# Second block's mixer: token-major values, pool means on GpSimd, heads 0 and 1 first, a place for each head's attention weights

## What is computed

```python
h = rmsnorm(x, mix_norm[l])
p = h @ w_in[l]                                   # 1024 -> 2048
a, f = p[..., :256], p[..., 256:512]              # pool, Fourier
q = p[..., 512:1024]; k = p[..., 1024:1536]       # 4 heads x 2 x 64
v = p[..., 1536:]                                 # 4 heads x 128

# pool: mean over a window of w in (2, 4, 8, 16) tokens for each 64 columns, minus the token itself
outs.append(win_sum / cnt - af[:, :, g])
y_pool = einsum('bsgc,gcd->bsgd', m, pool_w) * pool_scale
y_four = real(fft2(f)) @ fourier_w

# attention: per head two softmaxes, one taken from the other
s = q @ k.T * scale + bias;  p = softmax(s)
attn = p[:, :, 0] - lam * p[:, :, 1]
o = rmsnorm(attn @ v, head_norm) * (1 - lam_init)
x = x + concatenate([y_pool, y_four, y_attn]) @ w_out[l]
```

## Time and profile before

| | us |
|---|---|
| median of 3 runs | 2000.82 |
| lowest, highest | 1999.59, 2001.75 |
| the profiled execution | 2000.95 |
| its span | 1999.1 |
| TensorE busy in the span | 1982.2 |
| VectorE, ScalarE, GpSimd busy | 1426.4, 1020.5, 138.3 |
| the two mixers of the second block (windows) | about 1251 to 1324, 1714 to 1787 |

### The profile page before, as it was taken

One profiled execution on the slowest core, in us unless ns is written; L12 is line 12 of the kernel. 1 busy time (PEld: TensorE's weight loads), 2 busy tenths in 40 slices (PEclk: granted clock), 3 DMA queues, 4 the chain that ended last, 5 costly groups with the idle time before them and its releaser, 6 DMA issues.

```text
span 1999.1 us, 42334 instructions
## 1 busy us (share of the span) xinstructions
PE 1982.2 (99%) x16184; PEld 1942.0 (97%) x16184; DVE 1426.4 (71%) x2593; ACT 1020.5 (51%) x1525; POOL 138.3 (7%) x175
## 2 busy tenths in 40 slices
PE   9999999999999999999999999999999999999998
PEld 9999989999999999899999999999999999999998
DVE  6764887886688768878868775667756775667763
ACT  4433686554455447765536444564445443555443
POOL 0001022000100011310010000000000000000000
PEclk9999999999999999999999999999999999999999
DMA  7454423545444544255553664435554555435554
GB/s 258 177 204 166 161 85 128 189 168 195 156 171 171 188 154 158 84 185 189 190 178 143 224 234 160 147 127 191 188 213 169 190 194 193 147 126 189 189 208 150
DMA packets 46830, 346.66 MB, mean 173 GB/s; under 512 B 5344, under 2 KB 6416, under 8 KB 9232
## 3 DMA queue, kind: packets, MB, share of 16 engines
q1 hardware_dynamic: 44416, 335.63, 46.4%
q0 software_dynamic: 2320, 9.74, 1.5%
HBM read 344.29 MB, written 1.07 MB: 173 GB/s over the span
## 4 chain that ended last, share of the span: by engine, by line
PE 88%; DVE 6%; ACT 3%; DVEq 1%; issue 1%; ACTq 0%; DMA 0%; SPq 0%
PE ps L580 28%; PE ps L582 28%; PE ps L581 28%; DVE w_lo L1882 2%; ACT w_hi L1211 1%; ACT scratch L1559 1%; ACT cst L1549 1%; DVE cst L2350 0%; PE ps L1111 0%; PE ps L1076 0%; DMA raw<-in_w_up 0%; PE ps L800 0%; DVE plain L1993 0%; DVE pj L2329 0%; DVE scratch L2296 0%
## 5 line engine op out<-in xcount | busy, mean ns | idle before, releaser
L1882 DVE TENSOR_TENSOR w_lo<-raw,w_hi 128x1024 fp32r<-128x1024 f32 (+1 forms) x582 | 747.0, 1310 | 170.8 <-ACT w_hi L1211 168.7
L1211 ACT ACTIVATE w_hi<-raw 128x1024 fp32r<-128x1024 f32 (+1 forms) x582 | 634.9, 1121 | 148.4 <-PE ps L582 135.7
L580 PE MATMUL ps<-x_hi,w_lo 128*128 128x256 f32 (+2 forms) x2416 | 691.3, 286 | 2.7 <-DVE x_lo L1969 1.4
L582 PE MATMUL ps<-x_hi,w_hi 128*128 128x256 f32 (+2 forms) x2416 | 684.5, 283 | 0.0
L581 PE MATMUL ps<-x_lo,w_hi 128*128 128x256 f32 (+2 forms) x2416 | 681.6, 282 | 0.0
L580 PEld LDWEIGHTS ps<-x_hi,w_lo 128*128 128x128 f32 x2416 | 454.9, 188 | 10.7 <-issue 6.5
L581 PEld LDWEIGHTS ps<-x_lo,w_hi 128*128 128x128 f32 x2416 | 454.7, 188 | 0.8
L582 PEld LDWEIGHTS ps<-x_hi,w_hi 128*128 128x128 f32 x2416 | 455.1, 188 | 0.0
L580 PE MATMUL ps<-hid_hi,w_lo 128*128 128x256 f32 (+1 forms) x1536 | 435.6, 284 | 0.7 <-DVE hid_lo L2080 0.4
L581 PE MATMUL ps<-hid_lo,w_hi 128*128 128x256 f32 (+1 forms) x1536 | 434.1, 283 | 0.0
L582 PE MATMUL ps<-hid_hi,w_hi 128*128 128x256 f32 (+1 forms) x1536 | 433.4, 282 | 0.0
(11 more groups left out here) (325 smaller groups left out, 1554.6 us busy)
## 6 DMA issues: line engine op xcount, KB each, us to landing
raw<-in_w_up SPq DMA_DIRECT2D x176, 1024.0 KB, 4.8
raw<-in_w_down SPq DMA_DIRECT2D x64, 1408.0 KB, 6.0
raw<-in_w_in SPq DMA_DIRECT2D x36, 1024.0 KB, 4.8
raw<-in_w_out SPq DMA_DIRECT2D x16, 1024.0 KB, 4.8
cst<-row_copy POOLq DMA_DIRECT2D x2, 1088.0 KB, 8.7
raw<-in_w_up SPq DMA_DIRECT2D x4, 512.0 KB, 6.6
cst<-in_consts POOLq DMA_DIRECT2D x1, 1537.5 KB, 7.1
prm<-in_prm POOLq DMA_DIRECT2D x2, 690.0 KB, 7.5
```

Of the source, the lines that this page charges most:

```text
L580: mm(dst, w_lo[:, j, cols], xa, start=first, stop=False)
L582: return mm(dst, w_hi[:, j, cols], xa, start=False, stop=last)
L1211: fn(w_hi[:, j, c], raw[:, j, c], ACT.Copy).then_inc(hi_done, 1)
L1882: v.tensor_tensor(w_lo[:, j, c], raw[:, j, c], w_hi[:, j, c].bitcast(F32), ALU.subtract)\
```

## The change

Four things, all in the second block's mixer:

1. **Values token-major.** `value_tokens(pair, i)` takes the tokens as the stationary operand (chunk k of 128 tokens) and 256 columns of the weights, two heads, as the moving one. Four such units of 24 matmuls take the place of blocks 10 to 13, and each result already has the tokens on the partitions. The 1/rms of a token is then a scalar for each partition; `rstd_columns` makes that column with two products of one row, and ScalarE's `value_tokens` applies it on the way out of PSUM. A pair of weight units is needed whole at its first product and given back whole after the second.
2. **Pool means on GpSimd.** `window_means(l)` builds sums of 2, 4, 8 and 16 tokens by doubling, in padded rows, multiplies by 1/count (`rcount`, in place of `band`) and subtracts the token. It runs behind the fold. The transposes, the banded products and the two copies between them are gone.
3. **Order.** Queries and keys of heads 0 and 1 are blocks 0 to 3, Fourier 4 and 5, heads 2 and 3 are 6 to 9, pool 10 and 11, values 12 to 15. The four lists are rewritten for that, and the output projection takes pool second.
4. **`attn_t` has four places**, one a head, in the part of the constants left free.

The core of the diff (`-` before, `+` after):

```diff
-F0, A0 = 0, 14
-Q, K, V = (2, 4, 6, 8), (3, 5, 7, 9), (10, 11, 12, 13)
-CAT_ORDER = (2, 3, 4, 5, 6, 7, 0, 1)
+F0, A0, V0 = 4, 10, 12
+Q, K, V = (0, 2, 6, 8), (1, 3, 7, 9), (12, 13, 14, 15)
+CAT_ORDER = (2, 3, 0, 1, 4, 5, 6, 7)
...
+                def rstd_columns():
+                    pe.wait_ge(std_ready, norm + (3 * DEPTH + 1))
+                    for i in range(2):
+                        last = mm(ps[:, 6, 508 + i:509 + i], rstd[0:1, P * i:P * i + P], con("one", 1, slice(0, 1)),
+                                  start=True, stop=True)
+                    last.then_inc(rstd_t.sem, 1)
+
+                def value_tokens(pair, i):
+                    n = V0 + 2 * pair
+                    turn, j, bank = turn0 + n // 4, (n // 2) % 2, (n + i) % IN_BANKS
...
+                    pe.wait_ge(lo_done, turn * 4 + (2 * j + 2))
+                    both_hi, both_lo = (w[:, j, 0:2 * W_NARROW].rearrange("p (u w) -> p u w", u=2) for w in (w_hi, w_lo))
+                    dst, t = ps[:, bank, 0:256], slice(P * i, P * i + P)
+                    for k in range(KD):
+                        c = slice(k * P, k * P + P)
+                        mm(dst, xt_hi[:, k, t], both_lo[:, :, c], start=k == 0, stop=False)
+                        mm(dst, xt_lo[:, k, t], both_hi[:, :, c], start=False, stop=False)
+                        last = mm(dst, xt_hi[:, k, t], both_hi[:, :, c], start=False, stop=k == KD - 1)
...
                 rms_mean_square(norm)
                 block(2)
                 block(3)
+                rstd_columns()
+                att_s(0)
                 block(4)
+                block(5)
+                att_s(1)
+                block(6)
                 feature_sums()
-                block(5)
-                att_s(0)
-                block(6)
+                block(7)
                 token_sums()
-                block(7)
-                att_s(1)
+                att_t(0)
                 block(8)
+                att_s(2)
                 block(9)
-                att_t(0)
-                att_s(2)
+                att_t(1)
                 block(10)
                 fourier_out()
+                att_s(3)
                 block(11)
-                att_s(3)
-                v_transposes(0)
-                block(12)
-                att_t(1)
+                value_tokens(0, 0)
+                att_t(2)
+                value_tokens(0, 1)
+                att_t(3)
+                value_tokens(1, 0)
                 att_o(0)
-                v_transposes(1)
-                block(13)
                 att_o(1)
-                v_transposes(2)
-                block(14)
-                att_t(2)
-                v_transposes(3)
+                value_tokens(1, 1)
+                pool_out()
                 mean_squares(0)
-                block(15)
-                att_o(2)
-                att_t(3)
...
-                return {1: a_transposes, 2: last_output, 3: last_means, 4: pool_out}
...
+                return {1: lambda: att_o(2), 2: lambda: att_o(3), 4: lambda: mean_squares(1)}
...
                 scale(8)
                 weights(11)
-                maxima(1)
+                maxima(2)
                 scale(9)
                 weights(12)
-                maxima(2)
+                difference(1)
                 scale(10)
                 weights(13)
-                difference(1)
+                maxima(3)
                 scale(11)
                 fourier_low()
                 weights(14)
-                maxima(3)
-                scale(12)
+                difference(2)
                 weights(15)
-                difference(2)
-                scale(13)
+                difference(3)
                 weights(16)
...
+            def window_means(l):
...
+                pool.wait_ge(proj2_ready.sem, proj2_ready.at(l, A0 + 2))
+                nc.gpsimd.tensor_tensor(two[:, :, 1:T1], a[:, :, 0:T1 - 1], a[:, :, 1:T1], ALU.add)
+                pool.drain()
+                nc.gpsimd.tensor_tensor(four[:, :, 2:T1 - 1], two[:, :, 1:T1 - 2], two[:, :, 3:T1], ALU.add)
+                pool.drain()
...
+                nc.gpsimd.tensor_tensor(eight[:, 4:T1 - 3], four[:, 1, 2:T1 - 5], four[:, 1, 6:T1 - 1], ALU.add)
...
+                nc.gpsimd.tensor_tensor(sixteen[:, 8:T1 - 7], eight[64:P, 4:T1 - 11], eight[64:P, 12:T1 - 3], ALU.add)
...
+                    nc.gpsimd.tensor_tensor(poolm[rows, :, :], sums[rows, :, inner], count, ALU.mult)
...
+                nc.gpsimd.tensor_tensor(poolm, poolm, a[:, :, inner], ALU.subtract).then_inc(pm_ready.sem, 1)
```

More of the change, by code:

```diff
@@ L452, in build @@
         attn = take(2, 2, T2)
-        atok = take(2, T2)
         used[0] = NF * T1 + KD * T2
         vtok = take(2, 512)
-        attn_t = take(2, 2, T2)
         sqo = take(4, T2)
         poolm = take(2, T2)
+        windows = [cst[:, CC["rest"] + 2 * T1 * i:CC["rest"] + 2 * T1 * (i + 1)].rearrange("p (a t) -> p a t", a=2)
+                   for i in range(2)]
+        attn_t = cst[:, CC["rest"] + 4 * T1:CC["rest"] + 4 * T1 + 8 * T2].rearrange("p (h k t) -> p h k t", h=ATT_HEADS, k=2)
+        assert CC["rest"] + 4 * T1 + 8 * T2 <= CC_W
         y_squares = scr[:, 14 * T2:22 * T2].rearrange("p (k t) -> p k t", k=KD)
@@ L1049, in window_means @@
[L1049 to L1059, removed]
@@ L2615, in mixer2 @@
                 weights(6)
+                maxima(0)
                 scale(4)
@@ L2619, in mixer2 @@
                 weights(8)
-                maxima(0)
+                maxima(1)
                 scale(6)
                 weights(9)
+                difference(0)
                 scale(7)
@@ L2658, in mixer2 @@
                 att_low(3)
-                pool_low()
+                weights(19)
             v.memset(rstd[:], 1.0).then_inc(ones_set, 1)
@@ L2776, in fold_tokens @@
                 nc.gpsimd.tensor_tensor(fold[:, 1, :, :], early_half, late_half, ALU.subtract).then_inc(folded.sem, 1)
+            def window_means(l):
+                two, four = windows
+                a = pj[:, A0:A0 + 2, :]
+                for pad in (slice(0, POOL_PAD), slice(POOL_PAD + T2, T1)):
+                    nc.gpsimd.memset(a[:, :, pad], 0.0)
+                pool.drain()
[3 more added lines that the diff above has]
+                nc.gpsimd.tensor_tensor(four[:, :, 2:T1 - 1], two[:, :, 1:T1 - 2], two[:, :, 3:T1], ALU.add)
+                pool.drain()
+                eight, sixteen = two[:, 1, :], four[64:P, 1, :]
+                nc.gpsimd.tensor_tensor(eight[:, 4:T1 - 3], four[:, 1, 2:T1 - 5], four[:, 1, 6:T1 - 1], ALU.add)
+                pool.drain()
+                nc.gpsimd.tensor_tensor(sixteen[:, 8:T1 - 7], eight[64:P, 4:T1 - 11], eight[64:P, 12:T1 - 3], ALU.add)
+                pool.drain()
+                inner = slice(POOL_PAD, POOL_PAD + T2)
+                for rows, sums in ((slice(0, 64), two), (slice(64, P), four)):
+                    count = con("rcount", 2 * T2, rows).rearrange("p (a t) -> p a t", a=2)
+                    nc.gpsimd.tensor_tensor(poolm[rows, :, :], sums[rows, :, inner], count, ALU.mult)
+                pool.drain()
+                nc.gpsimd.tensor_tensor(poolm, poolm, a[:, :, inner], ALU.subtract).then_inc(pm_ready.sem, 1)
             def spread_rows(l):
```

157 lines of the change are left out of this document (69 added, 88 removed).

## The result

The changed kernel takes 2020.88 us (median of 5 runs, 2019.99 to 2021.69), the kernel before 2000.82: a ratio of 1.0100 (95% interval 1.0090 to 1.0111), 20.1 us slower. The forecast said slower by 12.5 us, 2013.4, in a range of 2005 to 2020. The sign was right, the size was not, and the time lies outside the range. The profiled execution has a span of 2019.1 us.

The account below looks back on a forecast made before the run. TensorE, busy 1982.2 of 1999.1 us, was taken as the bound. Per layer -3.5 + 3.7 + 3.1 + 1.6 + 1.35 = +6.2, two layers +12.5 on 2000.95: 2013.4 us, range 2005 to 2020.

Parts of the forecast that it names:

- The work taken from TensorE: Second block's mixer: pool matmuls, transposes and a wait removed, two small products added; net -3.5 us a layer.
- The first wait: TensorE at att_t(1), right behind block 9, waits 3.7 us a layer for VectorE's difference(1).
- The second wait: TensorE at att_t(2), behind the first value unit: 1.5 us from the order, 3.1 with GpSimd collisions, up to 3.8.
- its last two wait for 5.0 and end at 5.85: Last two steps of VectorE's difference before att_t(2), held by GpSimd's 538-element add; us from block 11's last start.
- The difference's early steps pass beside it: VectorE's early difference steps before att_t(2) were to run beside GpSimd's 538-element add without being held.
- The third wait: TensorE at att_t(3), behind the next value unit, waits 1.6 us a layer for VectorE; 0 to 2.6.
- The fourth wait: Tail, output projection: TensorE waits 1.35 us a layer (1.2 to 1.6) for head 2's low part.
- rival (d): TensorE's clock falls to half rate after the 3.7 us waits, +2.8 us a layer: 2019 us; chance 0.09.
- (a): No collision: GpSimd falls into VectorE's gaps or gives way, +3.05 us a layer, 2007 us; chance 0.15.
- (b): TensorE's waits don't come and only the removed TensorE work counts: -7.0 us, 1994 us; chance 0.08.
- (c): Only the wait at att_t(1) is real, the others near none: +0.2 us a layer, 2001 us; chance 0.05.
- (e): The order does something else, such as GpSimd's chain late enough to hold pool_out: 2018 us or more; chance 0.03.

Follow-up runs that it names:

- e7: Changed kernel with att_t(1) behind the Fourier output, att_t(2) and att_t(3) behind the third and fourth value units, and no window sums; 1998.56 us.
- e8: Changed kernel with GpSimd's chain held until difference(3) is done, att_t(1) to att_t(3) later, output projection reordered to fit; 1993.89 us, ratio 0.9969.
- e2: Changed kernel with att_t(1) moved from behind block 9 to behind block 10 and the Fourier output; 2009.99 us.
- e9: Kernel of e8 with one line put back, att_t(1) behind block 9 as in the changed kernel; 2005.14 us.
- e10: Changed kernel with one edit, GpSimd's chain waits for difference(3); 2016.24 us.
- e5: Changed kernel with 8 and 9 throwaway matmuls put on TensorE before the waits of att_t(1) and att_t(2); 2016.75 us.
- e6: Changed kernel without the window sums, only the last of GpSimd's seven operations left, so the pool part is not computed; 2012.91 us.
- e3: Changed kernel with att_t(2) and att_t(3) moved later, behind the third and fourth value units; 2020.13 us.
- e4: Changed kernel with the moves of e2 and e3 together; 2010.05 us.

## Why the prediction was right and wrong

**The work taken from TensorE** (-3.5 a layer): right as far as the runs can tell. The profiled executions give 3.4 (e7) and about 3.45 (e8, span 1992.2 against 1999.1); the medians on one chip give 2.4 and 3.1. In it the value units are a little cheaper than assumed: 0.68 us for six starts (1301.61 to 1302.29) against 0.70 in the earlier trace rows.

**The first wait** (3.7): right in place and cause, shown by e2 and e9. It measured 3.89 in the first layer, where the difference ran 0.4 us longer than in the earlier trace rows, with 0.45 us of issue ahead of its second step, and 3.52 in the second, where it did not. That the two sum up to the forecast is in part luck.

**The second wait** (3.1, at most 3.8): right in place, undersized at 4.31, beyond the end of its range. The part that the order makes was right: 1.38 in e10 against 1.5. The collisions cost 2.9 and not 1.6. The failing step is "its last two wait for 5.0 and end at 5.85". Counted from block 11's last start (1301.49) they began at 4.93 and ended at 7.26, because a product of GpSimd came in between the two. "The difference's early steps pass beside it" was wrong too: the two scalings were held by GpSimd as well (0.80 and 0.98 us against 0.23 and 0.61), so letting only operations with two SBUF tensors collide was too narrow. That did not delay the last two steps against the forecast, since GpSimd's adds had been taken too long (2.9 ns an element would be 1.6 us for the one of 542; it takes 1.09 in e8).

**The third wait** (1.6): did not show, because TensorE reached att_t(3) late at half speed; e5, with the clock held up, has it at 1.54. The term was right for a kernel whose clock does not fall, but by errors that cancel: the split before difference(3) took 2.29 us and not 1.1, and the last two steps, which were to be held until 9.9, were not held (0.88 us).

**The fourth wait** (1.35): 1.33.

**The clock.** This is the main miss, and the step that failed: the sum puts what follows a long wait at full speed, a term of nothing, with no row that showed it. It stood as rival (d), with 0.09, and 2.8 us behind the first wait alone. It came behind both long waits, 1.55 and 2.6 us in the first layer, 1.5 and 1.4 in the second, 7.1 in all and 4.0 net of the third wait. The sum of the forecast and its errors: 12.5, plus 2.4 for the second wait, 7.1 for the clock, 0.2 for the work taken away, less 3.2 for the third wait, 19.0 of the 20.1 measured. The trace of before could not show the clock's part, as I wrote, and from "nothing shows what 3.7 us of idleness does" I went on to a small chance. The Trainium skill (TensorE: Matmul & The Clock Gate, Part 1 and "Why this matters for your kernels") says that TensorE falls back to half rate when it idles for long between bursts of matmuls. The traces agree, at waits of 3.52 to 4.31 us. By that rule the term belonged in the sum and not among the rivals.

**Rivals.** (a), no collision, fell with e6 and e10: the collisions are there and cost 2.9 us of the wait. (b) and (c), waits that don't come, fell with the first profile. (e): pool_out did not wait in the changed kernel; it does in e10.

## What to carry to other kernels

In a kernel whose instruction lists are written by hand, check each wait that a move creates by the last common event: what the other engine still has to do from there, counted in rows, against what this engine does in the meantime; one call between block 9 and block 10 cost 11 us. Give a long wait on TensorE two terms, one for itself and one for the slow clock behind it (1.4 to 2.6 us here behind waits of 3.5 to 4.3). Work given to GpSimd is not free for VectorE: put it beside a stretch of VectorE that nobody waits for, and move its reader with it.

## What the runs showed of the hardware

- The granted clock stayed at 1.00 behind TensorE waits of 1.38 (e10), 1.54 (e5), 1.81 (e10) and 1.86 us (e6), and fell to 0.50 behind those of 3.89, 4.31, 3.52 and 4.30 us in the changed kernel and of 3.90 and 3.91 us in e3, e4, e6, e9 and e10. No run has a wait between 1.86 and 3.51 us. How much the fall costs differs, 2.6 us behind 4.31 and 1.4 behind 4.30 in one execution. Where it begins differs too: in e10 the transposes and the first matmuls behind the wait still run at full speed, and the starts are 0.21 us apart only from 1292.60 on.
- A VectorE scaling of two elements by per-partition factors (L2561) waited for a GpSimd add, 0.80 us against 0.23; the reciprocal before it (L2559) did not, 0.16. Between two adjacent VectorE steps (L2566) a GpSimd product ran (1307.20), and the pair took 2.33 us against 0.88.
- GpSimd's adds cost less per element when they are long: 0.74 us for 256, 1.09 for 542.
